# The last pass of a hybrid decoder block: where the final norm's loads, squares and scales stand among the last weight chunks

## The chip, the cores and the metric

The kernel runs on one core of one Trainium2 chip. The metric is the device time of one execution in microseconds, of which several runs are taken. The profile shows one execution; its span runs from the first to the last instruction.

## What is computed

The reference is one decoder block: two mixers (a diagonal state space and an mLSTM) on a shared projection, then a mixture of 32 experts of which each token uses four, then a final RMS norm. What matters here is its end:

```
def rmsnorm(x, g):
    xf = x.astype(jnp.float32)
    y = xf * lax.rsqrt(jnp.mean(xf * xf, axis=-1, keepdims=True) + RMS_EPS)
    return (y * g.astype(jnp.float32)).astype(x.dtype)
...
        h = h + moe_ffn(rmsnorm(h, norm_ffn_g[l]), w_router[l], b_router[l], w_up[l], b_up[l],
                        w_down[l], b_down[l])
    return rmsnorm(h, norm_final_g)
```

There are 1024 tokens of 1024 values in float32, so the output is 4 MB, eight tiles of 128 tokens (512 KB each).

## The kernel before

The experts' stage is `experts`, written out by hand for each engine; the order of the code is the order of the instructions on each engine, and semaphores tie the engines together. The work goes in passes. A pass takes one or two blocks of up to 128 tokens of one expert and streams that expert's weights through in twelve chunks of 1 MB: chunks 0 to 7 are of `w_up`, 8 to 11 of `w_down`. Each chunk goes the same way:

- SP loads it into one of six raw slots (`load`, L2340 to L2342). Chunk j uses slot j mod 6, so its load waits until DVE has done with chunk j-6.
- ACT rounds it to the high part (`hi_ahead`, L2576 to L2579), one cast of 128x2048.
- DVE subtracts to get the low part (`lo`, L2709 to L2712).
- PE multiplies: twelve matmuls for a chunk of a pass of one block (`multiply`, L2901 on).

After chunk 7 DVE makes the second half of the hidden values (`hide`), PE transposes them, ACT (`h_high`, L2588) and DVE (`h_low`, L2736) split them, and PE needs both for chunks 10 and 11. ACT copies the outputs out of PSUM into `y` after chunk 10 and after chunk 11 (`y_out`, L2613). POOL adds `y` into the running result `h3` in HBM by an indirect DMA with addition (`scatter`, L2425).

The very last pass is of kind LAST, here with one block of tokens. It hides the final norm of the whole result beside its own matmuls: `h3` is complete but for that block's rows as soon as the scatter of the pass before it has landed (semaphores `y_free`). So in this pass:

- SP, after all chunk loads, loads the norm's gain and then the eight tiles of `h3` (`final_load`, L2344; `norm_all_but_last`, L2351). Tiles 0 to 3 have room of their own (`done_rows` and half of `bias_rows`), tiles 4 to 7 lie in the raw slots 0 and 1, and their loads wait until DVE has finished chunk 7.
- ACT squares and sums each tile (`square`, L2626), at steps j = 6, 7 and 8 of its loop.
- POOL makes the reciprocal roots, for tiles 0 to 3, 4 and 5, 6 and 7 (`power`, L2448; `BATCHES`, L2222).
- DVE scales each tile (`scale`, L2782) after the last chunk's work, SP stores it (`final_store`, L2347).
- The rows of the last block are handled apart: POOL fetches them into `x_rows` (L2474), DVE adds `y` (L2796), ACT squares (`square_row`), POOL makes the root, DVE scales (L2799), and POOL writes them over the stored output by an indirect DMA (L2496), which has to wait until all eight stores have landed. POOL also adds them to `h3` (`add_rows`, L2455), for the case that more work follows. With one block the second of these two additions goes to no row.

The loop of ACT's part, with the squares:

```
                        if j in (6, 8):
                            h_high(n, kind, j // 8, blocks, small)
                        ...
                        if j + SPLIT < CHUNKS or (kind is AHEAD and j < CHUNKS - 1):
                            hi_ahead(n, j + SPLIT)
                        ...
                        if kind is LAST and j in (6, 7, 8):
                            for t in range(4 if j == 8 else 2):
                                square(2 * j - 12 + t, 0)
```

Of the kernel before, what the change touches and what calls it, by code (L numbers as in the profile page):

```python
# [16 lines left out]
P = 128  # L17
T = 1024
D = 1024
TT = T // P  # L20
# [2106 lines left out]
def experts(nc, p, t_dram, h3_dram, keep, out):  # L2127

    with ExitStack() as ctx:
# [92 lines left out]
        BATCHES = [slice(0, 4), slice(4, 6), slice(6, 8)]  # L2222
# [111 lines left out]
        with nc.Block() as block:  # L2334
# [3 lines left out]
            def _(sp):  # L2338
# [12 lines left out]
                def norm_all_but_last(n, blocks):  # L2351
                    sp.wait_ge(bias_set, 1)
                    sp.dma_start(final_gain, p["norm_final_g"].rearrange("(a d) -> a d", a=1).to_broadcast([P, D])).then_inc(final_gain_in, 16)
                    for b in range(PAIR):
                        sp.wait_ge(y_free[b], n * 16 + 16)
                    for j in range(TT):
                        if j == 4:
                            sp.wait_ge(lo_done, n * CHUNKS + (LOW + RAW_USED))
                        final_load(j)
                    for j in range(TT):  # L2360
                        final_store(j, 0)
                    sp.wait_ge(stored, 16 * TT)
                    sp.wait_ge(rows_out, 16 * blocks)
                    sp.sem_inc(rows_written, 1)
# [9 lines left out]
                def one_pass(n, e, blocks, plan, kind=None, small=False):  # L2374
# [8 lines left out]
                    for j in range(EARLY, CHUNKS):  # L2383
                        load(n, e, j)
# [7 lines left out]
                sp.wait_ge(h3_out, 16 * TT)  # L2392
                last_passes(sp, one_pass)
# [9 lines left out]
            def _(pool):  # L2403
# [58 lines left out]
                def last_pass(n, at, second, turn, blocks):  # L2462
# [10 lines left out]
                    for b in range(blocks):  # L2473
# [3 lines left out]
                            bounds_check=last_token, oob_is_err=False).then_inc(back_in[b], 16)  # L2477
                    for i in range(len(BATCHES)):
                        power(i, 0)
# [7 lines left out]
                    add_rows(0, blocks)  # L2487
# [4 lines left out]
                    add_rows(1, blocks)  # L2492
# [75 lines left out]
            def _(act):  # L2568
# [72 lines left out]
                def item(n, kind, blocks, small=False):  # L2641
# [5 lines left out]
                    for j in range(CHUNKS):  # L2647
# [18 lines left out]
                        if kind is LAST and j in (6, 7, 8):  # L2666
                            for t in range(4 if j == 8 else 2):
                                square(2 * j - 12 + t, 0)
# [39 lines left out]
            def _(v):  # L2708
# [79 lines left out]
                def norm_all_but_last(n, blocks):  # L2788
                    v.wait_ge(final_gain_in, 16)
                    for j in range(TT):  # L2790
# [3 lines left out]
                    for b in range(blocks):  # L2794
                        v.wait_ge(back_in[b], 16)
                        v.tensor_tensor(x_rows[:, b, :], x_rows[:, b, :], y[:, b, :], ALU.add).then_inc(row_added, 1)  # L2796
                    v.wait_ge(row_rstd_set, 1)
# [4 lines left out]
                def item(n, kind, blocks, e, e_next, small=False):  # L2802
# [5 lines left out]
                    for j in range(CHUNKS):  # L2808
# [8 lines left out]
                        if j == 9 and kind is AHEAD:  # L2817
                            choose(n + 1, e_next)
                        if j + SPLIT < CHUNKS or (kind is AHEAD and j < CHUNKS - 1):
# [235 lines left out]
```

## Time and profile before

| | us |
|---|---|
| median of 3 runs | 2228.87 (2227.93 to 2231.86) |
| the profiled execution | 2227.35 |
| its span | 2225.6 |
| PE busy | 2126.1 (96% of the span) |
| DVE busy | 1610.5 (72%) |
| ACT busy | 1211.4 (54%) |
| POOL busy | 587.9 (26%) |

The last pass is the piece from 2170 us to the end. Busy shares of the whole span say nothing about it: PE is busy there until 2207 us and has no more work after that. All times below are microseconds from the start of the span. PE is TensorE, DVE VectorE, ACT ScalarE, POOL GpSimd, SP SyncE; SPq and POOLq rows are the issues of DMAs by these engines.

### The profile page before, as it was taken

To read this page: it belongs to the slowest core of one execution; us is meant where nothing else is said; L and a number is where in the kernel's file an instruction comes from. 1 tells how busy PE (TensorE), PEld (TensorE's weight loads), DVE (VectorE), ACT (ScalarE), POOL (GpSimd) and SP (SyncE) were. 2 spreads that over 40 slices of the span, in tenths; PEclk is the share of its full clock that TensorE was granted. 3 is DMA by queue.
4 is the path that set the end of the run, shared out by engine and by line. 5 is a ranking of instruction groups with operands and counts; after the bars stand their busy time and mean duration, and the time that the engine had idled before them with its cause. 6 is when DMAs were issued, how large, how long until landed. Compare 5 with 4: busy or idle time off the path is not lost.

```text
span 2225.6 us, 33282 instructions
## 1 busy us (share of the span) xinstructions
PE 2126.1 (96%) x10402; PEld 1765.4 (79%) x10403; DVE 1610.5 (72%) x1858; ACT 1211.4 (54%) x1251; POOL 587.9 (26%) x589
## 2 busy tenths in 40 slices
PE   7999987997899999999999999999999999999996
PEld 6887987686588888888888878887888888878785
DVE  4688977447855665778698675977976887677766
ACT  4423262331545554666577564757755676565655
POOL 1001031106511111334053050513511252131404
PEclk9999999997899999999999999999999999999998
DMA  7123275512976765979699795988986898777967
GB/s 186 58 86 139 86 164 190 185 57 86 351 260 215 226 223 179 338 246 373 228 359 378 233 331 180 362 284 286 364 310 224 284 369 308 244 244 282 309 238 271
DMA packets 287303, 541.66 MB, mean 243 GB/s; under 512 B 37302, under 2 KB 53798, under 8 KB 286146
## 3 DMA queue, kind: packets, MB, share of 16 engines
q1 hardware_dynamic: 262866, 495.07, 63.9%
q0 software_dynamic: 24368, 45.72, 8.2%
q8 instruction: 37, 0.61, 0.1%
q14 instruction: 32, 0.26, 0.0%
HBM read 513.61 MB, written 65.13 MB: 260 GB/s over the span
## 4 chain that ended last, share of the span: by engine, by line
PE 55%; issue 6%; DVE 6%; ACT 3%; DMA 3%; ACTq 0%; DVEq 0%; POOL 0%; SPq 0%; POOLq 0%
PE ex_ps_l L2945 7%; PE ex_ps_l L2944 7%; PE ex_ps_g L2944 6%; PE ex_ps_g L2945 6%; PE ex_ps_y L2944 5%; PE ex_ps_y L2945 5%; PE ex_ps_l L2948 4%; PE ex_ps_g L2948 4%; PE ex_ps_y L2948 3%; DVE ex_w_lo L2711 3%; PE ex_ps_t L2882 2%; ACT ex_w_hi L2579 2%; DMA ex_late<-in_w_down_dram 2%; PE ex_ps_t L2892 2%; PE ex_ps_g L2954 1%
## 5 line engine op out<-in xcount | busy, mean ns | idle before, releaser
L2711 DVE TENSOR_TENSOR ex_w_lo<-ex_late,ex_w_hi 128x2048 fp32r<-128x2048 f32 x204 | 464.2, 2291 | 222.5 <-ACT ex_w_hi L2579 154.7
L2411 POOL TENSOR_TENSOR ex_passed<-keep_ident 128x1 f32<-128x1 f32 x136 | 125.7, 924 | 1102.2 <-ACT ex_y L2622 1077.9
L2579 ACT CAST ex_w_hi<-ex_late 128x2048 fp32r<-128x2048 f32 x170 | 324.5, 1909 | 115.7 <-PE ex_ps_g L2945 60.7
L2711 DVE TENSOR_TENSOR ex_w_lo<-keep_sig_o,ex_w_hi 128x2048 fp32r<-128x2048 f32 x136 | 309.6, 2288 | 100.1 <-ACT ex_w_hi L2579 100.1
L2579 ACT CAST ex_w_hi<-keep_sig_o 128x2048 fp32r<-128x2048 f32 x134 | 255.1, 1904 | 120.6 <-PE ex_ps_l L2945 37.0
L2944 PE MATMUL ex_ps_l<-ex_w_hi,ex_x_hi 128*128 128x512 f32 x784 | 308.6, 394 | 2.0 <-DVE ex_w_lo L2711 2.0
L2944 PE MATMUL ex_ps_g<-ex_w_hi,ex_x_hi 128*128 128x512 f32 x784 | 306.5, 391 | 3.8 <-DVE ex_w_lo L2711 2.1
L2945 PE MATMUL ex_ps_l<-ex_w_lo,ex_x_hi 128*128 128x512 f32 x784 | 305.5, 390 | 0.0
L2945 PE MATMUL ex_ps_g<-ex_w_lo,ex_x_hi 128*128 128x512 f32 x784 | 305.1, 389 | 0.0
L2944 PE MATMUL ex_ps_y<-ex_w_hi,ex_h_hi 128*128 128x512 f32 x544 | 217.3, 400 | 1.2 <-DVE ex_h_lo L2747 0.9
L2945 PE MATMUL ex_ps_y<-ex_w_lo,ex_h_hi 128*128 128x512 f32 x544 | 212.1, 390 | 0.0
L2948 PE MATMUL ex_ps_l<-ex_w_hi,ex_x_lo 128*128 128x512 f32 x544 | 212.1, 390 | 0.0
L2948 PE MATMUL ex_ps_g<-ex_w_hi,ex_x_lo 128*128 128x512 f32 x544 | 211.7, 389 | 0.0
L2711 DVE TENSOR_TENSOR ex_w_lo<-keep_weights,ex_w_hi 128x2048 fp32r<-128x2048 f32 x68 | 155.6, 2289 | 27.9 <-ACT ex_w_hi L2579 24.8
L2944 PEld LDWEIGHTS ex_ps_g<-ex_w_hi,ex_x_hi 128*128 128x128 f32 x784 | 147.2, 188 | 34.4 <-issue 2.5
L2944 PEld LDWEIGHTS ex_ps_l<-ex_w_hi,ex_x_hi 128*128 128x128 f32 x784 | 147.2, 188 | 33.6 <-DVE ex_w_lo L2711 4.1
L2945 PEld LDWEIGHTS ex_ps_g<-ex_w_lo,ex_x_hi 128*128 128x128 f32 x784 | 147.2, 188 | 30.0
L2945 PEld LDWEIGHTS ex_ps_l<-ex_w_lo,ex_x_hi 128*128 128x128 f32 x784 | 147.3, 188 | 29.6
L2948 PE MATMUL ex_ps_y<-ex_w_hi,ex_h_lo 128*128 128x512 f32 x424 | 165.8, 391 | 0.0
L2579 ACT CAST ex_w_hi<-keep_weights 128x2048 fp32r<-128x2048 f32 x67 | 127.7, 1905 | 10.8 <-PE ex_ps_l L2945 7.7
L2944 PEld LDWEIGHTS ex_ps_y<-ex_w_hi,ex_h_hi 128*128 128x128 f32 x544 | 102.2, 188 | 23.2 <-DVE ex_h_lo L2747 3.7
L2948 PEld LDWEIGHTS ex_ps_l<-ex_w_hi,ex_x_lo 128*128 128x128 f32 x544 | 102.1, 188 | 21.5
(507 smaller groups left out, 4114.2 us busy)
## 6 DMA issues: line engine op xcount, KB each, us to landing
keep_sig_o<-in_w_up_dram SPq DMA_DIRECT2D x102, 1024.0 KB
ex_late<-in_w_up_dram SPq DMA_DIRECT2D x102, 1024.0 KB
ex_late<-in_w_down_dram SPq DMA_DIRECT2D x102, 1024.0 KB
keep_weights<-in_w_up_dram SPq DMA_DIRECT2D x68, 1024.0 KB
keep_sig_o<-in_w_down_dram SPq DMA_DIRECT2D x34, 1024.0 KB
st_tab<-tabs SPq DMA_DIRECT2D x8, 1408.0 KB, 12.4
keep_weights<-in_w_in_dram SPq DMA_DIRECT2D x5, 1024.0 KB, 5.5
pr_late_pieces<-in_w_in_dram SPq DMA_DIRECT2D x5, 1024.0 KB
```

The costliest lines, as they stand in the source:

```text
L2411: pool.tensor_tensor(passed[:, :], ident[:, 0:1], ident[:, 0:1], ALU.add).then_inc(passed_done, 1)
L2579: nc.scalar.copy(w_hi[:, j % SPLIT, :, :], raw(j)).then_inc(hi_done, 1)
L2711: v.tensor_tensor(w_lo[:, j % SPLIT, :, :], raw(j), w_hi[:, j % SPLIT, :, :].bitcast(F32), ALU.subtract).then_inc(lo_done, 1)
L2882: mm = pe.transpose(to[:, k * P:(k + 1) * P], x_rows[:, b, (4 * half + k) * P:(4 * half + k + 1) * P], ident[:, :])
L2892: mm = pe.transpose(to[:, k * P:(k + 1) * P], hidden[:, row(half, b, blocks), k * P:(k + 1) * P], ident[:, :])
L2944: pe.matmul(to[:, :], hi_in[:, b, kk, :], w_hi[:, s, k, :], start=first, stop=False)
L2945: mm = pe.matmul(to[:, :], hi_in[:, b, kk, :], w_lo[:, s, k, :], start=False, stop=last and b > 0)
L2948: mm = pe.matmul(to[:, :], lo_in[:, b, kk, :], w_hi[:, s, k, :], start=False, stop=last)
L2954: mm = pe.matmul(to[:, :], pick[:, b, :], bias_hl[:, col:col + 512], start=False, stop=True)
```

## The change

Five edits, all in the pass of kind LAST:

1. SP waits for `y_free` and issues the loads of tiles 0 to 3 between chunk 9 and chunk 10, ahead of the last two chunks of weights. Tiles 4 to 7 follow after chunk 11.
2. The gain is loaded before the last expert's passes, and not behind the last chunk.
3. The roots are made on two tiles at a time, in four batches. ACT squares tiles 0 and 1 at j = 6, tiles 2, 3 and 4 at j = 7, and 5, 6 and 7 at j = 8.
4. DVE scales tile 0 ahead of the last chunk's subtraction, tiles 1 to 5 after the second `h_low`, then adds the last rows, then scales tiles 6 and 7.
5. POOL's addition to no row moves from behind the root of the last rows to ahead of all roots.

```
-        BATCHES = [slice(0, 4), slice(4, 6), slice(6, 8)]
+        BATCHES = [slice(0, 2), slice(2, 4), slice(4, 6), slice(6, 8)]
...
                 def norm_all_but_last(n, blocks):
-                    sp.wait_ge(bias_set, 1)
-                    sp.dma_start(final_gain, p["norm_final_g"].rearrange("(a d) -> a d", a=1).to_broadcast([P, D])).then_inc(final_gain_in, 16)
-                    for b in range(PAIR):
-                        sp.wait_ge(y_free[b], n * 16 + 16)
-                    for j in range(TT):
-                        if j == 4:
-                            sp.wait_ge(lo_done, n * CHUNKS + (LOW + RAW_USED))
+                    sp.wait_ge(lo_done, n * CHUNKS + (LOW + RAW_USED))
+                    for j in range(4, TT):
                         final_load(j)
...
                     for j in range(EARLY, CHUNKS):
+                        if kind is LAST and j == CHUNKS - 2:
+                            for b in range(PAIR):
+                                sp.wait_ge(y_free[b], n * 16 + 16)
+                            for t in range(4):
+                                final_load(t)
                         load(n, e, j)
...
                 sp.wait_ge(h3_out, 16 * TT)
+                sp.wait_ge(bias_set, 1)
+                sp.dma_start(final_gain, p["norm_final_g"].rearrange("(a d) -> a d", a=1).to_broadcast([P, D])).then_inc(final_gain_in, 16)
                 last_passes(sp, one_pass)
...
+                    if blocks == 1:
+                        add_rows(1, blocks)
                     for i in range(len(BATCHES)):
                         power(i, 0)
...
-                    add_rows(0, blocks)
+                    for b in range(blocks):
+                        add_rows(b, blocks)
...
-                    add_rows(1, blocks)
                     pool.wait_ge(row_done, blocks)
...
                         if kind is LAST and j in (6, 7, 8):
-                            for t in range(4 if j == 8 else 2):
-                                square(2 * j - 12 + t, 0)
+                            for t in ((0, 1), (2, 3, 4), (5, 6, 7))[j - 6]:
+                                square(t, 0)
...
                 def norm_all_but_last(n, blocks):
-                    v.wait_ge(final_gain_in, 16)
-                    for j in range(TT):
+                    for j in range(1, 6):
                         scale(j, 0)
...
                         v.tensor_tensor(x_rows[:, b, :], x_rows[:, b, :], y[:, b, :], ALU.add).then_inc(row_added, 1)
+                    for j in range(6, TT):
+                        scale(j, 0)
...
+                        if kind is LAST and j == 7:
+                            v.wait_ge(final_gain_in, 16)
+                            scale(0, 0)
                         if j + SPLIT < CHUNKS or (kind is AHEAD and j < CHUNKS - 1):
                             lo(n, j + SPLIT)
```

How that stands on the engines. First the order of SP at the end of the last pass, before; `ex_late<-in_w_down_dram` are chunks 9, 10 and 11, `h` is `h3`, `ex_done_rows` holds tiles 0 to 2, `ex_bias_rows` tile 3 in one half and the gain in the other:

```order
L2342 DMA ex_late<-in_w_down_dram 128x4x512
L2341 REGISTER_ALU
L2342 DMA ex_late<-in_w_down_dram 128x4x512
L2341 REGISTER_ALU
L2342 DMA ex_late<-in_w_down_dram 128x4x512
L2353 DMA ex_bias_rows<-in_norm_final_g_dram 128x1024
L2355 ISA
L2345 DMA ex_done_rows<-h 128x1024 x3
L2345 DMA ex_bias_rows<-h 128x1024
L2358 REGISTER_ALU
L2345 DMA keep_weights<-h 128x1024 x2
L2345 DMA keep_sig_o<-h 128x1024 x2
```

And the same place in the changed kernel:

```order
L2342 DMA ex_late<-in_w_down_dram 128x4x512
L2381 ISA
L2345 DMA ex_done_rows<-h 128x1024 x3
L2345 DMA ex_bias_rows<-h 128x1024
L2341 REGISTER_ALU
L2342 DMA ex_late<-in_w_down_dram 128x4x512
L2341 REGISTER_ALU
L2342 DMA ex_late<-in_w_down_dram 128x4x512
L2352 REGISTER_ALU
L2345 DMA keep_weights<-h 128x1024 x2
L2345 DMA keep_sig_o<-h 128x1024 x2
```

Four tiles (2 MB) and a wait (L2381) stand now ahead of chunks 10 and 11, and the gain is gone from here.

ACT in the last pass, before, from the cast of chunk 10 to the first copy of `y` (the two `ex_w_hi` rows are the casts of chunks 10 and 11, L2593 is the second `h_high`, L2630 rows are squares):

```order
L2579 CAST ex_w_hi<-ex_late 128x2048
L2630 ACTIVATE ex_under,ex_mean<-ex_done_rows 128x1024 x2
L2578 REGISTER_ALU
L2579 CAST ex_w_hi<-ex_late 128x2048
L2630 ACTIVATE ex_under,ex_mean<-ex_done_rows 128x1024
L2630 ACTIVATE ex_under,ex_mean<-ex_bias_rows 128x1024
L2592 REGISTER_ALU
L2593 ACTIVATE ex_h_hi<-ex_ps_t 128x512
L2630 ACTIVATE ex_under,ex_mean<-keep_weights 128x1024 x2
L2630 ACTIVATE ex_under,ex_mean<-keep_sig_o 128x1024 x2
```

And in the changed kernel:

```order
L2583 CAST ex_w_hi<-ex_late 128x2048
L2634 ACTIVATE ex_under,ex_mean<-ex_done_rows 128x1024 x2
L2582 REGISTER_ALU
L2583 CAST ex_w_hi<-ex_late 128x2048
L2634 ACTIVATE ex_under,ex_mean<-ex_done_rows 128x1024
L2634 ACTIVATE ex_under,ex_mean<-ex_bias_rows 128x1024
L2634 ACTIVATE ex_under,ex_mean<-keep_weights 128x1024
L2596 REGISTER_ALU
L2597 ACTIVATE ex_h_hi<-ex_ps_t 128x512
L2634 ACTIVATE ex_under,ex_mean<-keep_weights 128x1024
L2634 ACTIVATE ex_under,ex_mean<-keep_sig_o 128x1024 x2
```

One more square, that of tile 4, stands ahead of the second `h_high`.

DVE in the changed kernel, from the last two subtractions on (L2715); before, the eight L2785 scales stood together ahead of the addition of the last rows (now L2799):

```order
L2715 TENSOR_TENSOR ex_w_lo<-ex_late,ex_w_hi 128x2048
L2751 SCALAR_TENSOR_TENSOR ex_h_lo<-ex_ps_t,ex_h_hi 128x512
L2789 SCALAR_TENSOR_TENSOR ex_done_rows<-ex_done_rows,ex_rstd,ex_bias_rows 128x1024 x2
L2789 SCALAR_TENSOR_TENSOR ex_bias_rows<-ex_bias_rows,ex_rstd 128x1024
L2789 SCALAR_TENSOR_TENSOR keep_weights<-keep_weights,ex_rstd,ex_bias_rows 128x1024 x2
L2799 TENSOR_TENSOR keep_x_rows<-keep_x_rows,ex_y 128x1024
L2789 SCALAR_TENSOR_TENSOR keep_sig_o<-keep_sig_o,ex_rstd,ex_bias_rows 128x1024 x2
L2804 SCALAR_TENSOR_TENSOR keep_x_rows<-keep_x_rows,ex_row_rstd,ex_bias_rows 128x1024
```

The scales of tiles 6 and 7 (`keep_sig_o`) come behind the addition, which needs the last block's `y`.

## Rows read from the trace of the kernel before

**Rows 1.** Chain of waits, 2180 us to the end: start, length, what held it

```profile
2182.85 11.59 DMA ex_done_rows<-h
...
2210.96 6.87 DMA out_dram<-keep_sig_o
...
2218.64 1.03 POOL out_dram L2496
```

**Rows 2.** Timeline of SP: start, length, line, what is issued, how many

```profile
2176.58 4.89 SPq L2342 DMA_DIRECT2D ex_late<-in_w_down_dram  x3
...
2182.47 1.37 SPq L2345 DMA_DIRECT2D ex_done_rows<-h  x3
2183.90 0.64 SPq L2345 DMA_DIRECT2D ex_bias_rows<-h  x1
...
2209.77 1.57 SPq L2349 DMA_DIRECT2D out_dram<-keep_sig_o  x2
```

**Rows 3.** Timeline of ACT; in brackets its idle time before and who ended it

```profile
2099.79 1.90 ACT L2579 CAST ex_w_hi<-keep_weights 128x2048 fp32r<-128x2048 f32 x1
...
2190.83 1.92 ACT L2579 CAST ex_w_hi<-ex_late 128x2048 fp32r<-128x2048 f32 x1 [0.17 <-PE ex_ps_l L2948]
2192.65 1.06 ACT L2630 ACTIVATE ex_under<-ex_done_rows 128x1024 f32<-128x1024 f32 x1
...
2194.47 1.06 ACT L2630 ACTIVATE ex_under<-ex_done_rows 128x1024 f32<-128x1024 f32 x1 [0.67 <-DMA ex_done_rows<-h]
...
2195.53 1.89 ACT L2579 CAST ex_w_hi<-ex_late 128x2048 fp32r<-128x2048 f32 x1
2197.32 1.05 ACT L2630 ACTIVATE ex_under<-ex_done_rows 128x1024 f32<-128x1024 f32 x1
...
2198.55 1.07 ACT L2630 ACTIVATE ex_under<-ex_bias_rows 128x1024 f32<-128x1024 f32 x1
...
2199.61 0.58 ACT L2593 ACTIVATE ex_h_hi<-ex_ps_t 128x512 fp32r<-128x512 f32 x1
...
2206.81 0.69 ACT L2622 ACTIVATE ex_y<-ex_ps_y,ex_scatter_at 128x512 f32<-128x512 f32 x1 [1.28 <-PE ex_ps_y L2948]
```

**Rows 4.** Timeline of DVE, last pass

```profile
2193.01 2.28 DVE L2711 TENSOR_TENSOR ex_w_lo<-ex_late,ex_w_hi 128x2048 fp32r<-128x2048 f32 x1
...
2208.46 2.47 DVE L2785 SCALAR_TENSOR_TENSOR keep_sig_o<-keep_sig_o,ex_rstd,ex_bias_rows 128x1024 f32<-128x1024 f32 x2
2210.86 1.22 DVE L2796 TENSOR_TENSOR keep_x_rows<-keep_x_rows,ex_y 128x1024 f32<-128x1024 f32 x1
2214.27 1.28 DVE L2799 SCALAR_TENSOR_TENSOR keep_x_rows<-keep_x_rows,ex_row_rstd,ex_bias_rows 128x1024 f32<-128x1024 f32 x1 [2.20 <-POOL ex_row_rstd L2491]
```

**Rows 5.** Timeline of PE: the second transposes and the start of chunk 10

```profile
2196.74 0.66 PE L2892 MATMUL ex_ps_t<-keep_ident,ex_lin 128*128 128x128 f32 x4 [0.28 <-DVE ex_lin L2776]
2201.03 0.50 PE L2944 MATMUL ex_ps_y<-ex_w_hi,ex_h_hi 128*128 128x512 f32 x1 [0.87 <-DVE ex_h_lo L2747]
```

**Rows 6.** Timeline of POOL, last pass

```profile
2181.06 2.27 POOL L2411 TENSOR_TENSOR ex_passed<-keep_ident 128x1 f32<-128x1 f32 x1 [5.46 <-DMA h<-ex_y,ex_scatter_at]
...
2208.77 2.52 POOL L2457 DMA_INDIRECT h<-ex_y,ex_scatter_at  x1 [0.17 <-issue]
2213.66 0.58 POOL L2491 TENSOR_TENSOR ex_row_rstd<-ex_row_mean,ex_neg_half 128x1 f32<-128x1 f32 x1
2214.43 2.62 POOL L2457 DMA_INDIRECT h<-ex_y,keep_nowhere  x1 [0.19 <-issue]
```

**Rows 7.** Busy time by stretch: engines PE, PEld, DVE, ACT, POOL, then clock, DMA share, GB/s

```profile
2084.00:2090.00 6.00, 6.00 (x30) 5.00 (x29) 5.96 (x6) 4.12 (x4) 5.39 (x4) 1.00 1.02 354
2192.00:2195.00 3.00, 3.00 (x15) 2.49 (x14) 3.00 (x3) 2.33 (x4) 0.00 (x0) 1.00 1.03 408
```

**Rows 8.** DMA issues, stores of tile 0 and of tile 6: KB, us to landing

```profile
out_dram<-ex_done_rows SPq DMA_DIRECT2D x1, 512.0 KB, 2.8
...
out_dram<-keep_sig_o SPq DMA_DIRECT2D x1, 512.0 KB, 5.1
```

## The prediction, as put on record before the changed kernel ran

> **What bounds the kernel now.** I read the chain of waits first, then the timelines of the five engines in the last pass, then the landings of single DMAs. The chain ends in the last indirect store on POOL at 2218.64, which is held by the landing of the store of tile 7: 6.87 us from its issue at 2210.96, so 2217.83 [rows 1]. That store was issued as soon as DVE had scaled tiles 6 and 7 [rows 4]. So three things set the end: when tile 7 is scaled, how long its store takes to land, and the indirect store behind it. The last rows themselves are ready earlier: DVE scales them at 2214.27 to 2215.55 [rows 4], which leaves 2.3 us to 2217.83.
>
> Before that there is a race among engines. PE waits 0.87 us for `h_low` before chunk 10 [rows 5], and `h_low` waits for the second `h_high`, which ACT starts at 2199.61, behind the squares of tiles 2 and 3 [rows 3]. So at that point ACT is what PE waits for. PE asked for its second transposes at 2196.74 and could have had `h_high` from about 2197.4 [rows 5]; two squares kept ACT from it. The last `y_out` ends at 2207.50 [rows 3]; I call that moment Y.
>
> One more row is to be seen before any sum: the stretch 2192 to 2195 has a DMA share of 1.03 and 408 GB/s [rows 7]. The DMA engines are full, so the order in which SP issues is the order in which things land, and one tile of 512 KB takes 524 KB / 408 GB/s = 1.28 us.
>
> **Edit 1, the loads.** Before, chunk 10 is the second of three issues that begin at 2176.58 and end at 2181.47, chunk 11 the third [rows 2]. Each waits for one subtraction of 2.28 us, so chunk 10 goes out near 2178.8. Now SP waits for `y_free` ahead of it. POOL waited for the same semaphores until 2181.06 [rows 6], so this wait is new for SP: it costs 2.3 us. Then come four issues, which took 2182.47 to 2184.54 [rows 2], 2.1 us. Chunk 10 is issued near 2183.2, 4.4 us later, and stands behind 2 MB. Queued behind SP's wait are chunk 11 and the loads of tiles 4 to 7; ACT waits for the chunks.
>
> When does chunk 10 land? Tile 1 landed at 2182.85 + 11.59 = 2194.44 [rows 1]. From chunk 10 on, chunk 10, chunk 11, the gain and tiles 0 and 1 were ahead of that moment: 3.5 MB. Now tiles 0 to 3 and chunk 10 are: 3 MB, 1.28 us less, so 2193.2. Bounds: if the queue is empty when tile 0 is issued at 2181.2, a 512 KB transfer in an empty queue took 2.8 us [rows 8] and five more pieces take 6.4 us: 2190.4. At the other end the queue runs dry for one piece's time while SP waits: 2194.5. I take 2193.2, since it comes from a row with the same queue, with the last rows' indirect fetch in it too. The Trainium skill (DMA: Bandwidth & Descriptors, "Anatomy of one DMA") gives a DMA about 2 us plus its bytes at 436 GB/s. By that estimate the 3 MB would land at 2190.4 as well, and the hold below would be nothing; no row here shows a read queue that quick.
>
> Before, ACT cast chunk 10 at 2190.83, released by PE and not by the load [rows 3]. The hold is 2193.2 - 2190.83 = 2.4 us, between 0 and 3.7. ACT works in order, so both squares, chunk 11, the next squares and `h_high` all move by it.
>
> **Edit 3, the squares.** From the cast of chunk 10 to `h_high` ACT took 2199.61 - 2190.83 = 8.78 us. Now a third square stands between the cast of chunk 11 and `h_high`: one square is 2198.55 - 2197.32 = 1.23 us [rows 3]. Against that the squares of tiles 0 and 1 stood 1.82 us apart with a wait for a load in it [rows 3]; now both tiles have long landed, so 0.59 us is saved. Sum +0.64 us. The second `h_high` starts at 2199.61 + 2.4 + 0.6 = 2202.6, chunk 10 at 2204.0, and Y moves by 3.0 us to 2210.5. The path by DVE is shorter: it subtracted chunk 10 at 2193.01 [rows 4], now at about 2195.1, so the transposes come 2.1 us later and PE's chunk 9 still ends ahead of 2202.6.
>
> **Edit 4, the scales.** Tiles 0 to 5 are scaled before Y: six of 1.24 us, with the roots made for them in time. Then DVE adds the last rows, 1.22 us, and scales tiles 6 and 7, 2.47 us [rows 4]. Tile 7 is stored at Y + 3.8 = 2214.3. Before it was 2210.96, so +3.3 us. This is the step where the change pays for its gains: the last store now depends on Y, and it did not before.
>
> What is gained is the queue. Before, seven stores were issued within eight microseconds ahead of the last, and POOL's addition to `h3` at 2208.77 lay among them [rows 6]; tile 6's store took 5.1 us and tile 7's 6.87 [rows 1, 8], where tile 0's took 2.8. Now six stores are out and nearly drained when tile 6's is issued at 2213.0, but the addition to `h3` starts at Y + 1.27 = 2211.8 and is beside the last two. Bounds: 2.8 and 6.87. I take 5.1, the row of a store with the addition just begun. That is -1.8 us. The store of tile 7 lands at 2219.4, +1.5 us. The Trainium skill's fit (same page and section) gives 2.0 + 1.2 = 3.2 us for a store of 512 KB. By this estimate the sum would be 0.4 below no change; the row of tile 0 agrees with it, those of tiles 6 and 7, taken in the state that counts here, do not.
>
> The last rows: POOL is busy with the addition until Y + 3.8, the root takes 0.58 us plus its predecessor, DVE scales for 1.28, ready at about Y + 6.4 = 2216.9 [rows 4, 6]. That is under 2219.4, so this path stays covered, by 2.5 us.
>
> **Edits 2 and 5.** The gain's 512 KB now come at the start of a stretch, 2084 to 2090, with a DMA share of 1.02 [rows 7]: 1.28 us in the queue ahead of the next pass's chunk 0. ACT casts that chunk at 2099.79, with no wait for a load [rows 3]. So ten microseconds of PE's work on the pass before cover it: nothing, and if that cover were gone, 1.28 us. The issue to no row took POOL 2.62 us [rows 6] and ended at 2217.05, just before POOL was wanted at 2217.83: it was hidden, and now it stands where POOL idles. Nothing.
>
> **Sum.** +3.3 - 1.8 = +1.5 us against the profiled 2227.35: 2228.9. The median of the three runs is 1.5 above the profiled execution, so in terms of runs I write 2228.87 + 1.5 = 2230.4. Ends: no hold and a landing of 2.8 give 0.64 + 0.3 - 4.1 = -3.1; a hold of 3.7 and a landing of 6.87 give 3.7 + 0.6 + 0.3 = +4.6.
>
> **Rivals.**
> *Chunk 10 lands in time and the end gets earlier.* If the queue is quick enough to bring it by 2190.8, Y moves by only 0.6 us and the end by -0.9 with a landing of 5.1, by -3.1 with 2.8: 2228.0 to 2225.8, say 2227. For it: the queue was partly served by slow additions until 2181, and these may finish sooner. Against it: the tile that landed at 2194.44. Chance 0.28.
> *Chunk 10 lands so late that the kernel gets slower by more than 0.2%.* Every microsecond after 2190.8 goes through ACT's queue one to one to Y and to the last store. From 2196 on, with a landing of 5.1, the end is 4.5 us later: 2233.5. It needs the tiles' 2 MB to flow at some 300 GB/s rather than 408, with the indirect fetch of the last rows taking its share in the same microseconds. With a landing of 6.87 it decides already at 2194.4. Chance 0.12.
> *The change does nothing.* The hold and the quicker queue cancel, and the end goes by the last rows: Y + 6.4 with Y at 2210.5 to 2211.5, that is within 1 us of before. It is the neighbour of my case, 0.1, at 2228.9.
> My own case, some 0.5 to 3 us later, has 0.5.
>
> **Numbers.** A measurement can tell about 0.2%, 4.5 us. Nearly all of these cases lie inside it: same 0.82. Faster needs more than 4.5 us, beyond the lower end: 0.06, for runs that scatter. Slower is the second rival: 0.12. The range runs from the first rival's lower part, 2226.0, to 2234.0.
>
> **What would show it.** In the changed profile: SP's first tile load near 2181.2 and chunk 10's near 2183.2; a wait of ACT's cast of chunk 10 for a DMA of `in_w_down_dram`, ended near 2193; the second `h_high` near 2202.6; PE's wait before chunk 10 grown from 0.87 to some 2 us, or a new one at its second transposes; `y_out` ending near 2210.5; the store of tile 7 issued 3.8 us after that and landing in about 5 us. Wrong would be: no DMA wait in front of that cast (first rival), a last store that lands in under 3.5 us, or a chain whose end goes through the last rows' root instead of the store.

## The result, and the profile after

| | before | after |
|---|---|---|
| median of 19 runs | 2227.98 (2226.17 to 2231.86) | 2233.64 (2228.88 to 2239.38) |
| the profiled execution | 2227.35 | 2235.17 |
| its span | 2225.6 | 2233.4 |
| PE busy | 2126.1 | 2131.9 |

The ratio is 1.0023, with a 95% interval of 1.0016 to 1.003: slower by some 5.1 us (3.6 to 6.7); the two medians are 5.7 us apart. The interval leaves out no change, and the 4.5 us (0.2%) that the prediction took as its limit lie inside it. The forecast said +1.5 us. The sign held, and so did the range, near its upper end. The size was three times too small. The measured time is that of the second rival, in which chunk 10 lands late.

The two profiled executions differ by 7.8 us, and not all of that is the change. The clock by stretch tells them apart. First the changed kernel (columns as in [rows 7]: engines PE, PEld, DVE, ACT, POOL, then clock, DMA share, GB/s):

```profile
600.00:620.00 20.00, 17.40 (x78) 14.15 (x77) 15.20 (x13) 11.71 (x11) 2.13 (x1) 0.91 1.05 386
685.00:705.00 20.00, 18.02 (x77) 14.57 (x76) 5.81 (x7) 9.03 (x10) 8.38 (x12) 0.91 0.77 217
2174.00:2180.00 6.00, 4.83 (x14) 3.85 (x15) 2.22 (x3) 3.25 (x4) 2.84 (x3) 0.72 0.71 194
```

The same stretches of the kernel before:

```profile
600.00:620.00 20.00, 16.88 (x85) 13.85 (x84) 16.00 (x15) 14.26 (x13) 2.18 (x2) 1.00 1.05 386
685.00:705.00 20.00, 18.16 (x85) 14.86 (x84) 8.35 (x8) 9.36 (x11) 8.27 (x12) 1.00 0.71 198
2174.00:2180.00 6.00, 6.00 (x28) 4.95 (x28) 5.71 (x3) 5.42 (x5) 1.56 (x1) 1.00 1.01 214
```

The first two clock dips lie where both kernels have the same code. They shift everything that follows. (A value between 0.50 and 1.00 is the mean of a stretch in which both levels occur.) So from here on I count from **S, the start of PE's first matmul of the last pass**: 2170.30 before, 2175.17 after:

```profile
2170.30 0.49 PE L2944 MATMUL ex_ps_g<-ex_w_hi,ex_x_hi 128*128 128x512 f32 x1 [2.09 <-DVE ex_w_lo L2711]
...
2175.17 0.69 PE L2952 MATMUL ex_ps_g<-ex_w_hi,ex_x_hi 128*128 128x512 f32 x1 [2.03 <-DVE ex_w_lo L2715]
```

The first row is of before, the second of the changed kernel. Over the twelve profiles of this study, whose code is the same up to the last expert, S lay anywhere from 2168.8 to 2177.4, without a tie to what was edited; the changed kernel itself, profiled once more, has it at 2168.8. So 4.9 us of the 7.8 are scatter.

What is left, from S to the end, grew from 55.3 to 58.2 us. SP's timeline, answering to [rows 2]:

```profile
2186.14 1.38 SPq L2345 DMA_DIRECT2D ex_done_rows<-h  x3
2187.57 0.43 SPq L2345 DMA_DIRECT2D ex_bias_rows<-h  x1
2188.12 1.05 SPq L2342 DMA_DIRECT2D ex_late<-in_w_down_dram  x2
...
2218.40 1.53 SPq L2349 DMA_DIRECT2D out_dram<-keep_sig_o  x2
```

ACT's, answering to [rows 3]:

```profile
2198.54 1.92 ACT L2583 CAST ex_w_hi<-ex_late 128x2048 fp32r<-128x2048 f32 x1 [1.41 <-DMA ex_late<-in_w_down_dram]
...
2207.98 0.58 ACT L2597 ACTIVATE ex_h_hi<-ex_ps_t 128x512 fp32r<-128x512 f32 x1
...
2215.17 0.69 ACT L2626 ACTIVATE ex_y<-ex_ps_y,ex_scatter_at 128x512 f32<-128x512 f32 x1 [1.88 <-PE ex_ps_y L2956]
```

PE's, answering to [rows 5]:

```profile
2204.24 0.66 PE L2900 MATMUL ex_ps_t<-keep_ident,ex_lin 128*128 128x128 f32 x4 [1.30 <-DVE ex_lin L2780]
...
2209.40 0.50 PE L2952 MATMUL ex_ps_y<-ex_w_hi,ex_h_hi 128*128 128x512 f32 x1 [1.73 <-DVE ex_h_lo L2751]
```

And the chain of waits, answering to [rows 1]:

```profile
2188.12 10.33 DMA ex_late<-in_w_down_dram
...
2219.60 6.56 DMA out_dram<-keep_sig_o
...
2226.98 1.07 POOL out_dram L2500
```

The picture is the one forecast: ACT waits for chunk 10's DMA, PE waits at both places, the last store is issued 3.7 us after Y (the end of the last `y_out`, 2215.86), and the end hangs on its landing. But this execution understates the hold. Its clock dip at the start of the last pass made PE some 1.6 us late for everything, and as much of the hold was hidden behind it. An execution without that dip is wanted.

### The profile page after: what moved, and what is told of

It is laid out like the page before. It is cut to its first block, busy times and chain, and to the rows that moved or that the text cites. A ratio compares the mean times of both kernels' runs of the same rounds, so it can differ in the third digit from the quotient of the medians.

```text
span 2233.4 us, 33285 instructions
## 1 busy us (share of the span) xinstructions
PE 2131.9 (95%) x10402; PEld 1769.3 (79%) x10403; DVE 1610.9 (72%) x1858; ACT 1211.1 (54%) x1251; POOL 589.6 (26%) x591
## 4 chain that ended last, share of the span: by engine, by line
PE 54%; issue 6%; DVE 6%; DMA 3%; ACT 3%; ACTq 1%; DVEq 0%; POOLq 0%; POOL 0%; SPq 0%
PE ex_ps_l L2953 7%; PE ex_ps_l L2952 7%; PE ex_ps_g L2952 6%; PE ex_ps_g L2953 6%; PE ex_ps_y L2952 5%; PE ex_ps_y L2953 5%; PE ex_ps_l L2956 4%; PE ex_ps_g L2956 4%; PE ex_ps_y L2956 4%; DVE ex_w_lo L2715 3%; DMA ex_late<-in_w_down_dram 3%; PE ex_ps_t L2890 2%; ACT ex_w_hi L2583 2%; PE ex_ps_t L2900 2%; PE ex_ps_g L2962 1%
## 5 line engine op out<-in xcount | busy, mean ns | idle before, releaser
L2715 DVE TENSOR_TENSOR ex_w_lo<-ex_late,ex_w_hi 128x2048 fp32r<-128x2048 f32 x204 | 464.2, 2290 | 224.9 <-ACT ex_w_hi L2583 154.0
L2715 DVE TENSOR_TENSOR ex_w_lo<-keep_sig_o,ex_w_hi 128x2048 fp32r<-128x2048 f32 x136 | 309.7, 2289 | 101.2 <-ACT ex_w_hi L2583 101.2
L2715 DVE TENSOR_TENSOR ex_w_lo<-keep_weights,ex_w_hi 128x2048 fp32r<-128x2048 f32 x68 | 155.7, 2289 | 28.2 <-ACT ex_w_hi L2583 25.1
L2952 PEld LDWEIGHTS ex_ps_y<-ex_w_hi,ex_h_hi 128*128 128x128 f32 x544 | 102.7, 189 | 24.2 <-DVE ex_h_lo L2751 4.6
L2956 PEld LDWEIGHTS ex_ps_g<-ex_w_hi,ex_x_lo 128*128 128x128 f32 x544 | 102.9, 189 | 21.6
```

Source lines behind the costliest of these rows:

```text
L2715: v.tensor_tensor(w_lo[:, j % SPLIT, :, :], raw(j), w_hi[:, j % SPLIT, :, :].bitcast(F32), ALU.subtract).then_inc(lo_done, 1)
L2952: pe.matmul(to[:, :], hi_in[:, b, kk, :], w_hi[:, s, k, :], start=first, stop=False)
L2956: mm = pe.matmul(to[:, :], lo_in[:, b, kk, :], w_hi[:, s, k, :], start=False, stop=last)
```

## The experiments

One table for all profiles, in us after S. "Store 7" is the chain's issue of tile 7's store and its time to landing; "last" is the final indirect store; the end is the end of the span. Ratios are against the kernel before, timed on the same chip, with 95% intervals.

| kernel | cast of chunk 10 | second `h_high` | Y | store 7 | last | end | ratio |
|---|---|---|---|---|---|---|---|
| before | 20.5 | 29.3 | 37.2 | 40.7 + 6.87 | 48.3 | 55.3 | |
| after | 23.4 | 32.8 | 40.7 | 44.4 + 6.56 | 51.8 | 58.2 | 1.0023 |
| after_again | 25.4 | 34.8 | 43.0 | 46.7 + 6.53 | 54.1 | 60.5 | 1.0021 [1.0005, 1.0036] |
| loads_behind | 20.5 | 30.0 | 37.9 | 41.6 + 6.61 | 49.0 | 55.4 | 0.9988 [0.9977, 0.9999] |
| scales_ahead | 24.6 | 34.0 | 41.9 | 43.8 + 4.83 | 49.5 | 56.5 | 0.9997 [0.9987, 1.0007] |
| after_no_add | 25.5 | 35.0 | 43.1 | 46.8 + 3.24 | 50.9 | 57.2 | 1.0003 [0.9992, 1.0013] |
| two_tiles_ahead | 21.7 | 31.4 | 39.3 | 43.0 + 6.60 | 50.5 | 56.9 | 1.0001 [0.9989, 1.0014] |
| one_tile_ahead | 20.6 | 31.2 | 40.7 | 44.5 + 6.60 | 51.9 | 58.3 | 1.0012 [1.0002, 1.0021] |
| loads_alone | 25.1 | 33.3 | 41.7 | 44.6 + 7.86 | 53.3 | 59.7 | 1.0007 [0.9997, 1.0016] |
| before_no_add | 20.6 | 29.1 | 37.0 | 40.5 + 5.04 | 46.3 | 52.9 | 0.9982 [0.9973, 0.9991] |
| best_two_after | 20.6 | 28.8 | 36.9 | 40.7 + 3.58 | 45.1 | 51.4 | 0.9975 [0.9965, 0.9985] |
| best_one_after | 20.5 | 28.7 | 36.9 | 40.6 + 3.53 | 44.9 | 51.4 | 0.9972 [0.9961, 0.9984] |

### The changed kernel once more

No edit.

> The changed kernel as it is, a second time. In the first profile of it the last pass began at 2175.2 us against 2170.3 before, so 4.9 us of the difference came before any changed instruction but one load; PE's granted clock dipped there in three short places (near 610, 690 and 2176 us). Theory A (chance: the dips fall where they fall in each execution): the start of the last pass comes out elsewhere than 2175.2, by some us. Theory B (the changed program is slower upstream too): again 2174 to 2176. Both expect the last pass, from PE's first matmul in it to POOL's last indirect store, to take 50 to 52 us (51.8 in the first profile, 1.6 of it by a dip; 48.3 before), with ACT waiting for chunk 10's DMA.

S is at 2168.8, so the later start of the first profile was scatter (Theory A). The pass up to the last indirect store took 54.1 us, more than the 50 to 52 expected. The end is at 60.5, 5.2 us after that of before, which fits the 5.1 us of the ratio. ACT's timeline:

```profile
2194.13 1.90 ACT L2583 CAST ex_w_hi<-ex_late 128x2048 fp32r<-128x2048 f32 x1 [4.97 <-DMA ex_late<-in_w_down_dram]
...
2203.55 0.58 ACT L2597 ACTIVATE ex_h_hi<-ex_ps_t 128x512 fp32r<-128x512 f32 x1
...
2211.07 0.69 ACT L2626 ACTIVATE ex_y<-ex_ps_y,ex_scatter_at 128x512 f32<-128x512 f32 x1 [1.88 <-PE ex_ps_y L2956]
```

The hold is in full view: 4.97 us of waiting, the cast 4.8 us later after S than before. Why so long? SP's timeline:

```profile
2179.91 2.22 SPq L2345 DMA_DIRECT2D ex_done_rows<-h  x3
2182.17 0.43 SPq L2345 DMA_DIRECT2D ex_bias_rows<-h  x1
2182.72 1.39 SPq L2342 DMA_DIRECT2D ex_late<-in_w_down_dram  x2
```

The four issues took 2.7 us and not 2.1, and chunk 10 went out 1.05 us later after S than forecast. It landed 11.31 us after its issue, at S + 25.3, by the chain of waits:

```profile
2182.72 11.31 DMA ex_late<-in_w_down_dram
```

And the DMA engines were not full. Three stretches from S + 9 to S + 18:

```profile
2177.77:2180.77 3.00, 3.00 (x15) 2.49 (x14) 3.00 (x2) 1.96 (x2) 0.69 (x1) 1.00 0.83 297
2180.77:2183.77 3.00, 3.00 (x15) 2.49 (x14) 2.96 (x4) 2.19 (x2) 2.16 (x5) 1.00 0.86 275
2183.77:2186.77 3.00, 3.00 (x17) 2.51 (x16) 3.00 (x2) 1.81 (x3) 2.69 (x2) 1.00 0.86 292
```

The same stretches of the kernel before:

```profile
2179.30:2182.30 3.00, 3.00 (x15) 2.50 (x14) 3.00 (x2) 1.96 (x2) 1.24 (x1) 1.00 1.03 320
2182.30:2185.30 3.00, 3.00 (x15) 2.49 (x14) 2.96 (x4) 2.19 (x2) 2.52 (x5) 1.00 1.03 364
2185.30:2188.30 3.00, 3.00 (x17) 2.50 (x16) 3.00 (x2) 1.82 (x3) 2.46 (x1) 1.00 1.04 401
```

Here 0.66 MB less were moved, 3 x (1085 - 864) KB. Counted in the same way from S + 6 to the landing, it is 0.87 MB, or 2.1 us at 408 GB/s. The forecast had chunk 10 land at S + 22.9; with the missing bytes that is 25.0, and it landed at 25.3. Not all of this is the time in which SP waited. Of the 0.66 MB, 0.07 are missing in the first of the three stretches, 0.27 in the second and 0.33 in the third, and by then, from S + 13.8 on, all four tiles had been issued: 2 MB stood in the queue, and the share was still 0.86. Why the engines weren't full there is not shown.

PE stood idle meanwhile, and its clock fell. Its timeline:

```profile
2199.80 1.12 PE L2900 MATMUL ex_ps_t<-keep_ident,ex_lin 128*128 128x128 f32 x4 [4.86 <-DVE ex_lin L2780]
...
2201.14 0.63 PE L2953 MATMUL ex_ps_y<-ex_w_lo,ex_h_hi 128*128 128x512 f32 x1
2201.57 0.63 PE L2956 MATMUL ex_ps_y<-ex_w_hi,ex_h_lo 128*128 128x512 f32 x1
```

And two stretches, one while it worked again and one after its last work:

```profile
2200.00:2202.00 2.00, 2.00 (x8) 1.71 (x7) 2.00 (x2) 1.91 (x4) 0.00 (x0) 0.50 0.22 88
...
2216.00:2219.00 3.00, 0.00 (x0) 0.00 (x0) 1.29 (x1) 0.00 (x0) 0.66 (x2) 0.50 0.99 229
```

After an idle time of 4.86 us the granted clock is 0.50, the lower level of 1.2 GHz, and matmuls start 0.43 us apart instead of 0.23. From the first start to the last, the twelve matmuls of chunk 9 took 4.6 us instead of 2.6. ACT's three squares covered most of that: from `h_high` to Y it is 8.2 us, where before it was 7.9, so 0.3 us got through.

### Only the loads put back

```
                     for j in range(EARLY, CHUNKS):
-                        if kind is LAST and j == CHUNKS - 2:
-                            for b in range(PAIR):
-                                sp.wait_ge(y_free[b], n * 16 + 16)
-                            for t in range(4):
-                                final_load(t)
...
                 def norm_all_but_last(n, blocks):
+                    for b in range(PAIR):
+                        sp.wait_ge(y_free[b], n * 16 + 16)
+                    for t in range(4):
+                        final_load(t)
```

> The changed kernel with tiles 0 to 3 loaded behind chunk 11 again. My theory (the early tiles hold chunk 10): the DMA wait before ACT's cast of chunk 10 goes, PE's waits at the second transposes and at chunk 10 shrink from 1.3 and 1.7 us to under 0.5 and about 1.5, and the last y_out ends 2.5 to 3 us earlier after the pass's first matmul (40.7 us in the first profile of the changed kernel, 39.1 without its dip); the last pass takes 47 to 48 us. Rival (the order of loads is indifferent, ACT's extra square does it): at most 1 us.

```profile
2192.50 1.92 ACT L2582 CAST ex_w_hi<-ex_late 128x2048 fp32r<-128x2048 f32 x1 [0.17 <-PE ex_ps_l L2955]
...
2201.94 0.58 ACT L2596 ACTIVATE ex_h_hi<-ex_ps_t 128x512 fp32r<-128x512 f32 x1
```

ACT's timeline shows the cast again released by PE, 0.17 us of idle time, and 9.44 us from there to the second `h_high`: the forecast said 9.42 for the squares' new order. Y moved by 0.66 us. The whole kernel is level with before in the trace and 0.12% faster by its ratio. The last indirect store, at S + 49.0, came later than the 47 to 48 us expected, since tile 7's store still took 6.61 us to land. With Edits 2 to 5 in place Edit 1 carries the loss, and those four together lose nothing.

### The loads alone

The other half of the same question: the kernel before, with Edit 1 only (the gain stays behind chunk 11):

```
                     for j in range(EARLY, CHUNKS):
+                        if kind is LAST and j == CHUNKS - 2:
+                            for b in range(PAIR):
+                                sp.wait_ge(y_free[b], n * 16 + 16)
+                            for t in range(4):
+                                final_load(t)
                         load(n, e, j)
```

> The kernel before with nothing changed but the place of the loads of tiles 0 to 3, now ahead of chunk 10 (the gain is still loaded behind chunk 11). Theory (this edit alone costs what the whole change costs, or more): ACT waits about 5 us for chunk 10 and casts it at 25.0 to 25.6 us after the pass's first matmul against 20.5, PE waits 4 to 5 us at its second transposes and its granted clock falls there, the last y_out ends at 41.5 to 42.5 instead of 37.2, and the end is 4 to 5 us later than before. Rival (the other edits cost the most): the end is under 2 us later than before.

```profile
2195.96 1.91 ACT L2581 CAST ex_w_hi<-ex_late 128x2048 fp32r<-128x2048 f32 x1 [4.73 <-DMA ex_late<-in_w_down_dram]
```

The cast waits 4.73 us for chunk 10 and the trace ends 4.4 us later than that of before. Its ratio, however, is 1.0007, some 1.5 us, and its interval takes in no change. The profiled run was 1.7 us above the median of its own runs (2232.32 against 2230.64), which closes a part of the gap and not all. That the hold is there is shown. What it costs when the other edits are away is not settled: by the ratio's interval between nothing and some 3.6 us.

The last store in this kernel took 7.86 us, the longest of all:

```profile
2215.49 7.86 DMA out_dram<-keep_sig_o
```

### How many tiles ahead of chunk 10

```
                         if kind is LAST and j == CHUNKS - 2:
                             for b in range(PAIR):
                                 sp.wait_ge(y_free[b], n * 16 + 16)
-                            for t in range(4):
+                            for t in range(2):
                                 final_load(t)
...
                 def norm_all_but_last(n, blocks):
+                    for t in range(2, 4):
+                        final_load(t)
```

> The changed kernel with two tiles of the final norm ahead of chunk 10 instead of four. Counting from PE's first matmul of the last pass, ACT cast chunk 10 at 20.5 us with no tile ahead and at 25.4 us with four (no clock dip in the pass). Theory (the bytes ahead hold the chunk, besides the wait of SP for y_free): two tiles are 1 MB, 2.6 us less, so the cast starts at 22.5 to 23.2 us, and the end moves by about as much, 2 to 3 us earlier than the changed kernel. Rival (the wait for y_free and the gap it leaves in the queue is the price, not the bytes): the cast stays at 24.5 us or later.

And the same with `range(1)` and `range(1, 4)`:

> The changed kernel with one tile of the final norm ahead of chunk 10, and with SP's wait for y_free at the same place. Casts of chunk 10 so far: 20.5 us with none ahead and no wait there, 21.7 with two, 25.4 with four. Theory (bytes ahead are the price, the wait alone is covered): with one tile the chunk lands before 20.5 us and ACT waits for PE again, cast at 20.5 to 20.7. Rival (the wait is a good part): still a DMA wait in front of the cast, which starts at 21 us or later.

The cast starts at S + 20.5, 20.6, 21.7 and 25.4 with none, one, two and four tiles ahead. SP's wait for `y_free` stands in three of these, and with one tile the cast is not late, so the wait by itself doesn't hold chunk 10 beyond what its slack covers. The first two tiles cost the cast 1.1 us, less than the 2.0 to 2.7 expected, and the next two 3.7, more than their bytes (2.6 us at 408 GB/s). ACT's row with two tiles:

```profile
2193.97 1.91 ACT L2585 CAST ex_w_hi<-ex_late 128x2048 fp32r<-128x2048 f32 x1 [1.29 <-DMA ex_late<-in_w_down_dram]
```

With one tile the cast is right on time and the kernel is slower all the same. ACT's timeline there:

```profile
2189.54 1.92 ACT L2585 CAST ex_w_hi<-ex_late 128x2048 fp32r<-128x2048 f32 x1 [0.17 <-PE ex_ps_l L2958]
...
2193.84 1.06 ACT L2636 ACTIVATE ex_under<-ex_done_rows 128x1024 f32<-128x1024 f32 x1 [1.34 <-DMA ex_done_rows<-h]
```

And PE's:

```profile
2201.66 0.57 PE L2954 MATMUL ex_ps_y<-ex_w_hi,ex_h_hi 128*128 128x512 f32 x1 [2.76 <-DVE ex_h_lo L2753]
2202.02 0.63 PE L2955 MATMUL ex_ps_y<-ex_w_lo,ex_h_hi 128*128 128x512 f32 x1
2202.45 0.63 PE L2958 MATMUL ex_ps_y<-ex_w_hi,ex_h_lo 128*128 128x512 f32 x1
```

Tile 1 now stands behind chunks 10 and 11 and comes 1.34 us late for its square, and the square is ahead of `h_high` in ACT's order: the late load has only moved from the chunk to the tile. From S + 6 to S + 24 the DMA engines moved 320 GB/s here and 348 in loads_behind, 0.50 MB or 1.2 us less, though tile 1 stands behind the same 2.5 MB in both. So the wait ahead of the issues isn't free: chunk 10 had room for what it costs, tile 1 had not. PE then waits 2.76 us before chunk 10, and behind that the matmuls start 0.43 us apart. This time nothing covers them: `h_high` to Y takes 9.5 us instead of 7.9. With waits of 1.19 and 2.04 us at the two places (two_tiles_ahead), and of 1.53 us (loads_behind), it took 7.9, with no such fall. By the place of the cast alone the time should grow with the number of tiles, and at one tile it doesn't: the trace ends 1.4 us later than with two. Against none (loads_behind) the ratios show the loss, 1.0012 against 0.9988; against two, 1.0001, their intervals overlap.

### All scales ahead of the last rows

```
-                    for j in range(1, 6):
+                    for j in range(1, TT):
                         scale(j, 0)
...
-                    for j in range(6, TT):
-                        scale(j, 0)
```

> The changed kernel with tiles 6 and 7 scaled ahead of the addition of the last rows. My theory (the last store depends on Y only through this order): the last store is issued about 1.8 us earlier, since its root is ready 1.1 us before Y, and the end comes 1.5 to 2.5 us earlier. Rival (the end is set by the addition to h3 that shares the DMA engines with the last two stores, whenever they are issued): the landing time grows by as much as the issue gains, and the end stays within 0.5 us.

Store 7 went out 2.9 us earlier after S than in after_again, 1.1 of it because Y itself came earlier in this execution, and landed in 4.83 us. The end came 4.0 us earlier after S, 2.9 after Y, more than the 1.5 to 2.5 expected. But the end hung on something else. POOL's timeline:

```profile
2214.55 3.37 POOL L2459 DMA_INDIRECT h<-ex_y,ex_scatter_at  x1 [0.43 <-issue]
2217.67 0.54 POOL L2494 TENSOR_SCALAR ex_row_mean<-ex_row_mean 128x1 f32<-128x1 f32 x1
2218.30 0.58 POOL L2496 TENSOR_TENSOR ex_row_rstd<-ex_row_mean,ex_neg_half 128x1 f32<-128x1 f32 x1
2220.95 1.07 POOL L2500 DMA_INDIRECT out_dram<-keep_x_rows,ex_scatter_at  x1 [2.07 <-DVE keep_x_rows L2802]
```

The last indirect store is now released by DVE's scale of the last rows, whose root stood behind POOL's issue of the addition to `h3`. The store landed at 2220.12 and that scale ended at 2220.19, so the two paths are level here. Counted from Y, the last indirect store came 3.6 us earlier than in after_again (7.5 instead of 11.1 us): that much the place of the last two scales costs here, 1.85 us in the issue and 1.7 in the landing. The ratio went from 1.0021 to 0.9997 with it.

### The addition to h3 taken away

The additions to `h3`, and the wait for them, go under a condition. With one block of tokens in the last pass and no more work behind, the condition is false, so here they aren't made:

```
                     if blocks == 1:
-                        add_rows(1, blocks)
+                        with pool.If(most > SLOTS):
+                            add_rows(1, blocks)
...
-                    for b in range(blocks):
-                        add_rows(b, blocks)
+                    with pool.If(most > SLOTS):
+                        for b in range(blocks):
+                            add_rows(b, blocks)
```

> The changed kernel with POOL's additions to h3 in the last pass made only when more work follows, which it doesn't with these inputs; so they are left out, and nothing else. Theory (the addition by DMA delays the last store, 6.56 us to landing in the first profile against 2.8 for a lone one): landing 2.8 to 3.5 us, the last indirect store waits for the last rows instead, and the end comes 3 to 4 us earlier. Rival (a last store takes so long because of the two before it): landing stays over 5 us and the end moves by less than 1 us.

And the same done to the kernel before:

> The kernel before with POOL's two additions to h3 in the last pass made only when more work follows, so left out here. Theory (the addition delays the last stores): the store of tile 7 lands 4 to 5 us after its issue instead of 6.87, still with stores queued ahead of it, and POOL's last indirect store starts 1.5 to 2.5 us earlier than 48.3 us after the pass's first matmul. Rival (the queue of eight stores is the whole delay): under 0.5 us.

The chain's row of the last store, first of the changed kernel without the addition:

```profile
2217.46 3.24 DMA out_dram<-keep_sig_o
```

then of the kernel before without it:

```profile
2210.33 5.04 DMA out_dram<-keep_sig_o
```

The last indirect store still waits for the store of tile 7 in both, and not for the last rows, as I had expected for the first. With the store issued at the same place after Y, its landing falls from 6.53 to 3.24 us in the changed kernel, and from 6.87 to 5.04 in the kernel before. So in the kernel before, of the 3.6 us beyond those 3.24, 1.8 were the addition, and the other 1.8 are left for the seven stores close ahead, which no run takes away alone. In the changed kernel all 3.3 are the addition: Edit 4 did free the queue, and spent it on a worse overlap. The row of after_again's stretch 2216 to 2219 above shows that overlap: the share of the DMA engines is 0.99, and they move 229 GB/s.

### The parts that pay, together

Loads behind chunk 11 as before, no addition to `h3` here, four batches of roots with squares of tiles 0 and 1, 2 and 3, then 4 to 7, and the scale of tile 0 early. The core of it, against the changed kernel:

```
-                            for t in ((0, 1), (2, 3, 4), (5, 6, 7))[j - 6]:
+                            for t in ((0, 1), (2, 3), (4, 5, 6, 7))[j - 6]:
                                 square(t, 0)
...
-                    for j in range(1, 6):
+                    for j in range(1, 7):
                         scale(j, 0)
...
-                    for j in range(6, TT):
+                    for j in range(7, TT):
                         scale(j, 0)
```

> The same with tile 6 scaled ahead of the addition and only tile 7 behind it. Theory: the addition starts up to 1 us later, since DVE is busy with scales until about 38.3 us after the pass's first matmul, the store of tile 7 lands at about the same time, and the end is within 0.5 us of the version with two behind, because the last rows and the last store end together at 43 to 44 us. Rival: DVE still idles before the addition, and this one ends 1 us earlier.

And with tiles 6 and 7 both behind the last rows' addition, as in the change:

> What the runs so far speak for: the changed kernel with the tile loads behind chunk 11, ACT's second h_high behind four squares in all as before, the additions to h3 left out, and tiles 6 and 7 scaled behind the addition of the last rows. Theory: chunk 10 cast at 20.5 us after the pass's first matmul, second h_high at 28.8, last y_out ended at 37, store of tile 7 issued at 40.8 and landed 3.3 us later, the last indirect store at 44.5 to 45 us, against 48.3 before and 54.1 in the changed kernel: 3 to 4 us faster than before. Rival (the last rows' path takes over): 46 us or more, with the wait on the scaling of the last rows.

The chain of best_one_after:

```profile
2213.12 3.53 DMA out_dram<-keep_sig_o
...
2217.47 1.09 POOL out_dram L2502
```

Its last indirect store comes at S + 44.9, 3.4 us before that of before, and the runs give 0.9972 [0.9961, 0.9984]: 2224.15 against 2229.29. In the trace the end comes 3.9 us earlier. It is faster than before, and so than the changed kernel with its 1.0021. The two versions can't be told apart by their times. Against before_no_add (0.9982) the intervals overlap, so the gain over that is seen in the traces only (51.4 against 52.9).

## Why the prediction came out as it did

**The hold of chunk 10 was mis-sized: this is the step that failed.** The mechanism was right, the size of this term of the sum was not. The step read: "Now tiles 0 to 3 and chunk 10 are: 3 MB, 1.28 us less, so 2193.2". It carried the rate of a queue that was never short of work over to one that was. In the kernel before, SP issued chunks 9, 10 and 11 at S + 6.3, 8.5 and 10.8, so both last chunks were out by the time the additions had landed; now only chunk 9 was issued until the wait for `y_free` ended. The DMA engines moved 0.87 MB less, and chunk 10 came at S + 25.3 instead of 22.9. The hold is 4.8 us against 2.4 forecast. The upper bound, "runs dry for one piece's time", was S + 24.2 and was passed as well; the stretch before the wait ends, 4.3 us in which SP issues nothing, against one chunk in the queue beside slow additions, should have widened it. With one tile ahead 0.50 MB are missing against loads_behind; over a third of the 0.87 goes missing with all four tiles already issued (S + 15 to S + 18), and why is open. The size also varies: over the five profiles with four tiles ahead the cast came at S + 23.4 to 25.5, the least of them in the one with the clock dip, where PE itself asked for it later.

**By the Trainium skill's figure** (DMA: Bandwidth & Descriptors, "Anatomy of one DMA") there would have been no hold. That section gives it for one DMA issued by GpSimd, and these are several, issued by SP. No trace agrees: with 2 MB ahead ACT waited 4.97 us.

**The squares' order** was right to 0.02 us: 9.42 us in after_again and 9.44 in loads_behind, against 9.42.

**The last store's issue** at Y + 3.8 was right: Y + 3.7 in each of the profiles with this order.

**The last store's landing** was taken as 5.1 us, -1.8 against before. It is 6.53 in after_again, -0.3. The bounds held it, but the reason for the choice was wrong. I chose by the state of the queue of stores; what the runs show to count is how POOL's addition lies on the store. Where the store is issued 0.7 us behind the start of the addition's issue (scales_ahead) it takes 4.83 us, where 2.2 us behind (before, after_again) 6.87 and 6.53, and with no addition 3.24. (The 7.86 us of loads_alone, 1.75 us behind and with its other stores close ahead, are above all of these; one execution shows them.) The prediction's own times put it 2.5 us behind, 2214.3 against 2211.8, so the row to take was tile 7's and not tile 6's, which had been issued 1.0 us behind. The Trainium skill's 3.2 us (same page and section) is near what the store takes once the addition is gone (3.24 to 3.6 in three profiles), so there the trace agrees; with the addition beside it, it doesn't.

**The sum**, in after_again against before: +4.8 hold, +0.6 squares, +0.3 clock, +0.3 from Y to the issue, -0.3 landing, -0.5 behind the landing, together +5.2, as measured. Forecast was 2.4 + 0.6 + 0.3 - 1.8 = +1.5. That the range held is partly luck: its worst case was +4.6 us, less than the 5.1 measured. The measured 2233.64 lies inside because the upper end was written as 2234.0, and because the median of 19 runs of before is 0.9 us below that of the three from which the range was counted.

**The cover of the last rows** held: forecast were 2.5 us to spare, and in after_again DVE had scaled them at 2218.07, 3.9 us before the store landed at 2222.02. scales_ahead shows how near that is: with 3.6 us off the store's path they are level.

**Edits 2 and 5** at nothing: loads_behind contains both and isn't slower. No run has them alone, so a small cost could be hidden by Edits 3 and 4. But I put the gain's load in the wrong place. In the first profile of the change SP issues it at 2132.51, and not near 2084:

```profile
2132.51 0.35 SPq L2394 DMA_DIRECT2D ex_bias_rows<-in_norm_final_g_dram  x1
```

**The rivals.** "Chunk 10 lands so late" named the mechanism, 2 MB at some 300 GB/s (measured over S + 9 to S + 18: 275 to 297), and the price, 4.5 us. It had 0.12, and deserved more: the additions that slow the queue were in the rows, and I used them as an argument for the other rival. "Chunk 10 in time" is out: its sign, no DMA wait, is seen only with the tiles taken away or but one left.

## What to carry to other kernels

When a wait is put in front of issues on a queue, count what is still queued behind it: if that is less than the wait lasts, the transfers behind the wait are late not by the bytes ahead of them alone but also by what the engines failed to move meanwhile (0.50 MB here with one tile ahead, 0.87 with four). A late load is paid by whoever stands first in the order of the engine that needs it, so moving it behind something else moves the wait, and a part-way dose can be worse than none. And ask whether work near the end is needed at all in this case: here an addition that nobody reads cost 2.4 us in the traces, and the reorderings that pay gained 1.5.

## What the runs showed of the chip

An indirect addition of 512 KB beside a store takes far more than its bytes: 229 GB/s at a DMA share of 0.99, against 408 at 1.03 in [rows 7], and a store that lands in 3.24 us without it takes 6.5 (after_no_add and after_again).

PE's granted clock was 0.50 after it had idled 4.86 us. Behind waits of 4.10 (scales_ahead), 4.62 (loads_alone) and 5.03 us (after_no_add) in the same place, and behind one of 2.76 us (one_tile_ahead), its matmuls started 0.43 us apart too. Behind waits of 1.19, 1.53 and 2.04 us in the same pass they kept 0.23. At S it differed between executions: behind a wait of 2.03 us in the first profile of the change matmuls started 0.43 us apart for some 3 us (a mean clock of 0.72 over 2174 to 2180), behind one of 2.09 us in the kernel before they started 0.23 us apart, with the clock at 1.00. In some executions the clock also fell in stretches where the code is the same for all kernels (0.91 over 600 to 620, where before has 1.00). That scatter of some microseconds is as large as the effect, so two single profiles can't be compared by their spans; counted from the start of the stage, they can, as long as no dip falls inside it, as one did in the first profile of the change.
